# Up projection by channels with the norm root multiplied in the sums

## The reference

```python
h = rmsnorm(x, ffn_norm[l])                     # x: (1, 256, 2048)
u = causal_dwconv(jnp.einsum('bsd,df->bsf', h, w_up[l]), conv_w[l], conv_b[l])
gate, up = jnp.split(u, [D_FF], axis=-1)        # D_FF = 5632, w_up: (2048, 11264)
x = x + jnp.einsum('bsf,fd->bsd', jax.nn.silu(gate) * up, w_down[l])
```

## Time and profile before

| | us |
|---|---|
| median of 3 timed runs (2417.47 to 2429.39) | 2417.7 |
| profiled execution | 2424.76 |
| its span | 2423.0 |
| TensorE busy | 2336.9 |
| VectorE busy | 1652.8 |
| ScalarE busy | 1048.0 |
| one turn of the up loop, 569.3 to 665.8 | 96.5 |

### The profile page before, as it was taken

The page is one execution under the profiler, slowest core; times in us unless marked ns, Lnnn a source line. Parts: engine busy times, 40 slices in busy tenths (PEclk is TensorE's granted clock), DMA queues, the critical chain, the costliest instruction groups (busy, mean ns, idle before and its releaser), DMA issues.

```text
span 2423.0 us, 31984 instructions
## 1 busy us (share of the span) xinstructions
PE 2336.9 (96%) x11221; PEld 1935.5 (80%) x11221; DVE 1652.8 (68%) x2393; ACT 1048.0 (43%) x1506; POOL 75.1 (3%) x112
## 2 busy tenths in 40 slices
PE   8999999999999999999999999998999699899997
PEld 6778778878878788777888888887888699799976
DVE  5368866687787877777778585766758765466644
ACT  5576554555555555343452222223222625443433
POOL 1012110000000000000000000000000000000000
PEclk9999999999999999999999999999999899899999
DMA  7946544576766666777746464544646255312243
GB/s 242 196 149 197 178 133 154 175 233 200 234 210 216 223 219 207 237 246 239 250 157 208 140 197 142 183 155 157 224 159 219 79 180 172 113 61 74 69 145 133
DMA packets 225519, 430.39 MB, mean 178 GB/s; under 512 B 13799, under 2 KB 38623, under 8 KB 224128
## 3 DMA queue, kind: packets, MB, share of 16 engines
q1 hardware_dynamic: 222112, 418.96, 54.5%
q10 hardware_dynamic: 2720, 9.83, 1.2%
q0 software_dynamic: 576, 0.14, 0.0%
HBM read 426.16 MB, written 2.72 MB: 177 GB/s over the span
## 4 chain that ended last, share of the span: by engine, by line
PE 64%; issue 19%; DVE 7%; DMA 5%; ACT 4%; DVEq 0%; POOL 0%; SPq 0%; ACTq 0%; POOLq 0%
PE ps L600 38%; PE ps L634 11%; PE ps L611 9%; DMA raw<-in_w_down 3%; DVE lo L547 2%; ACT hi L543 2%; DVE ada_acc L576 2%; PE ps L650 1%; DVE ustage L1683 1%; DMA raw<-in_w_in 1%; PE ps L2295 1%; DMA xres<-in_x 1%; PE ps L2193 0%; PE ps L2045 0%; PE ps L2044 0%
## 5 line engine op out<-in xcount | busy, mean ns | idle before, releaser
L543 ACT ACTIVATE hi<-raw 128x1024 fp32r<-128x1024 f32 x604 | 635.6, 1059 | 1142.5 <-PE ps L600 540.6
L547 DVE TENSOR_TENSOR lo<-raw,hi 128x1024 fp32r<-128x1024 f32 x604 | 730.9, 1222 | 523.5 <-ACT hi L543 520.6
L576 DVE SCALAR_TENSOR_TENSOR ada_acc<-raw,csil,ada_acc 128x512 f32<-128x512 f32 x720 | 491.7, 746 | 2.4 <-DMA raw<-in_ada_w 2.4
L600 PE MATMUL ps<-hi,h_hi 128*128 128x512 f32 x960 | 383.0, 399 | 6.5 <-DVE lo L547 6.5
L600 PE MATMUL ps<-hi,h_lo 128*128 128x512 f32 x960 | 378.9, 395 | 0.0
L600 PE MATMUL ps<-lo,h_hi 128*128 128x512 f32 x960 | 378.8, 395 | 0.0
L600 PE MATMUL ps<-hi,g 128*128 128x512 f32 x704 | 227.8, 400 | 7.0 <-DVE lo L547 6.9
L600 PEld LDWEIGHTS ps<-hi,h_hi 128*128 128x128 f32 x960 | 180.8, 188 | 53.4 <-DVE lo L547 13.4
L600 PEld LDWEIGHTS ps<-hi,h_lo 128*128 128x128 f32 x960 | 180.8, 188 | 42.3
L600 PEld LDWEIGHTS ps<-lo,h_hi 128*128 128x128 f32 x960 | 181.0, 188 | 40.1
L600 PEld LDWEIGHTS ps<-hi,g 128*128 128x128 f32 x704 | 133.2, 189 | 43.0 <-DVE lo L547 12.0
(11 more groups left out here) (323 smaller groups left out, 3584.4 us busy)
## 6 DMA issues: line engine op xcount, KB each, us to landing
raw<-in_ada_w SPq DMA_DIRECT2D x192, 512.0 KB, 4.2
raw<-in_w_up SPq DMA_DIRECT2D x176, 512.0 KB, 4.5
raw<-in_w_down SPq DMA_DIRECT2D x88, 512.0 KB, 4.9
raw<-in_w_in SPq DMA_DIRECT2D x84, 512.0 KB, 4.4
raw<-in_pool_w_in SPq DMA_DIRECT2D x64, 512.0 KB, 4.1
raw<-in_mla_w_in SPq DMA_DIRECT2D x56, 448.0 KB, 3.9
raw<-in_w_out SPq DMA_DIRECT2D x32, 512.0 KB, 3.6
raw<-in_pool_w_out SPq DMA_DIRECT2D x32, 512.0 KB, 4.6
```

The lines of the kernel that those rows point to most:

```text
L543: act.activation(hi[:, slot, :, :], raw[:, slot, :, :], ACT.Copy).then_inc(hi_split, 1 + ada)
L547: dve.tensor_tensor(lo[:, slot, :, :], raw[:, slot, :, :], hi[:, slot, :, :].bitcast(F32), ALU.subtract).then_inc(lo_split, 1)
L576: ins = dve.scalar_tensor_tensor(acc, raw[:, slot, k, :], csil[:, v, kt:kt + 1], acc, ALU.mult, ALU.add)
L600: mm = pe.matmul(ps[:, bank, 0:n], a[:, kt0 + k, tok * P:(tok + 1) * P], w[:, slot, k, col0:col0 + n], start=first and k == 0 and s == 0, ...
```

## The change

The up projection keeps a 128x128 tile of the weights fixed and moves the 256 tokens of h: 24 matmuls of 256 columns a chunk. The result has channels on partitions, as the convolution needs it. Gate panels stay in banks 0 and 1 and up panels in 2 and 3 until their taps are done; a panel waits for the taps of the one before it in its banks. The staging and the transpositions are gone.

The norm root is needed as a row over tokens, the same on all partitions. VectorE makes two diagonal matrices from the root columns, TensorE multiplies them by a matrix of minus ones into bank 3 (before chunk 6 of gate panel 0), and VectorE copies that with the sign turned to `root_row`. Each finished panel is multiplied by it in place in PSUM (`scale_u`, one VectorE operation of 128x1024), and the taps read the scaled sums.

The down panels use banks 6, 0, 2, 0 (and the next), and the squares of the second norm of x go to a throw-away tile in SBUF.

```diff
+        root_diag = at(120)("root_diag", [P, TT, P])
+        root_row = at(128)("root_row", [P, SEQ])
+        x_junk = at(8)("x_junk", [P, W])
...
-        def turned_u(m):
-            return ps[:, 6 + m // 2, (m % 2) * SEQ:(m % 2 + 1) * SEQ]
+        def u_cols(which, m):
+            return ps[:, 2 * which + m // 2, (m % 2) * SEQ:(m % 2 + 1) * SEQ]
+        DOWN_BANKS = [6, 0, 2, 0]
...
+        def panel_by_channels(pe, first, i, order, j0, a_hi, a_lo, bank0, before=None):
+            for j in range(CH):
+                if before is not None:
+                    before(j0 + j)
+                at = first + place(order, j0 + j)
+                slot = at % RING
+                pe.wait_ge(lo_split, i * len(order) + at + RING + 1)
+                for k in range(CK_T):
+                    for n in range(W // P):
+                        for s, (w, a) in enumerate(((hi, a_hi), (hi, a_lo), (lo, a_hi))):
+                            mm = pe.matmul(ps[:, bank0 + n // 2, n % 2 * SEQ:(n % 2 + 1) * SEQ], w[:, slot, k, n * P:(n + 1) * P],
+                                           a[:, CK_T * j + k, :], start=j == 0 and k == 0 and s == 0 and n % 2 == 0,
+                                           stop=j == CH - 1 and k == CK_T - 1 and s == 2 and n % 2 == 1)
+                mm.then_inc(chunks_used, 1 + ada_behind(at))
...
-            def stage_u(n, which, used_chunks):
-                act.wait_ge(chunks_used, used_chunks)
-                act.wait_ge(g_lo_done, FREE + n) if which == 0 else act.wait_ge(gated, FREE + n)
-                for i in range(TT):
-                    ins = act.activation(ustage[:, which, i, :], ps[:, 2 * which + i, :], ACT.Identity, scale=x_stats(1)[2][:, i:i + 1])
-                ins.then_inc(u_staged[which], 1)
             def tap_two(i, which):
-                act.wait_ge(u_turned[which], i + 1)
+                act.wait_ge(u_scaled[which], i + 1)
+                act.wait_ge(g_lo_done, FREE + i) if which == 0 else act.wait_ge(gated, FREE + i)
...
-                stage_u(n, 1, done(CH))
...
-                    stage_u(n + 1, 0, done(2 * CH))
...
-                panel_squares(act, 2, i * 2, ps[:, 6, :])
+                panel_squares(act, 2, i * 2, x_junk[:, :])
...
+            def root_columns():
+                dve.wait_ge(x_root, 2)
+                for i in range(TT):
+                    dve.tensor_scalar(root_diag[:, i, :], ident, x_stats(1)[2][:, i:i + 1], None, ALU.mult).then_inc(root_diag_ready, 1)
+            def root_rows():
+                dve.wait_ge(root_spread, 1)
+                dve.tensor_scalar(root_row[:, :], ps[:, 3, 0:SEQ], -1.0, None, ALU.mult).then_inc(root_row_ready, 1)
+            def scale_u(which, used_chunks):
+                dve.wait_ge(chunks_used, used_chunks)
+                v = ps[:, 2 * which:2 * which + 2, :].rearrange("p a (b n) -> p (a b) n", n=SEQ)
+                dve.tensor_tensor(v, v, root_row[:, :].unsqueeze(1).to_broadcast([P, 4, SEQ]), ALU.mult).then_inc(u_scaled[which], 1)
...
                 older_taps(n, 0)
-                split(ahead(2), ahead(CH) if last else ahead(CH + 2))
+                split(ahead(2), ahead(CH))
+                scale_u(1, done(CH))
+                if not last:
+                    split(ahead(CH), ahead(CH + 2))
                 older_taps(n, 1)
...
                     split(ahead(CH + 4), ahead(2 * CH))
+                    scale_u(0, done(2 * CH))
...
-            los(dve, C_UP, 0, 0, 1 + RING, CH + RING)
+            los(dve, C_UP, 0, 0, 1 + RING, 4 + RING)
+            root_columns()
+            los(dve, C_UP, 0, 0, 4 + RING, CH + RING - 1)
+            root_rows()
+            los(dve, C_UP, 0, 0, CH + RING - 1, CH + RING)
+            dve.wait_ge(root_row_ready, 1)
+            scale_u(0, used(C_UP + CH))
...
             def gate_panel(n, first, i, order, j0, before=None):
-                pe.wait_ge(u_staged[0], FREE + n)
-                panel_by_tokens(pe, first, i, order, j0, h_hi, h_lo, pair(0), W, before=before)
+                pe.wait_ge(taps[0], FREE + n * 2)
+                panel_by_channels(pe, first, i, order, j0, h_hi, h_lo, 0, before)
...
+                if j == CH - 2:
+                    pe.wait_ge(root_diag_ready, TT)
+                    for i in range(TT):
+                        mm = pe.matmul(ps[:, 3, i * P:(i + 1) * P], negones, root_diag[:, i, :], start=True, stop=True)
+                    mm.then_inc(root_spread, 1)
...
+            pe.wait_ge(root_row_ready, 1)
...
-                        if j == j0 + CH + 2:
-                            turn_u(n, 1)
...
-            turn_u(N_UP - 1, 1)
...
+                    if i * 2 + half in (1, 2):
+                        pe.wait_ge(taps[2 - i * 2 - half], FREE + N_UP * 2)
+                    panel_by_tokens(pe, C_DOWN, i, DOWN_ORDER, half * n, g_hi, g_lo, [(tok, DOWN_BANKS[i * 2 + half] + tok) for tok in range(TT)],
+                                    W, FT, before=ada_before)
```

More of the change, by code:

```diff
@@ L518, in two_block_kernel @@
         attn_added, ffn_added = sem("attn_added"), sem("ffn_added")
-        u_staged = [sem("gate_staged"), sem("up_staged")]
-        u_turned = [sem("gate_turned"), sem("up_turned")]
+        u_scaled = [sem("gate_scaled"), sem("up_scaled")]
+        root_diag_ready, root_spread, root_row_ready = (sem(n) for n in ("root_diag_ready", "root_spread", "root_row_ready"))
         taps = [sem("gate_taps"), sem("up_taps")]
@@ L1152, in _ @@
             act.sem_inc(mla_taken, PAIR)
-            for s in (x_squared, u_staged[0], u_staged[1], g_hi_done):
+            for s in (x_squared, g_hi_done):
                 act.sem_inc(s, FREE)
@@ L1275, in _ @@
                     panel_squares(act, 1, n, x_squares[:, :])
-            def stage_u(n, which, used_chunks):
-                act.wait_ge(chunks_used, used_chunks)
-                act.wait_ge(g_lo_done, FREE + n) if which == 0 else act.wait_ge(gated, FREE + n)
-                for i in range(TT):
-                    ins = act.activation(ustage[:, which, i, :], ps[:, 2 * which + i, :], ACT.Identity, scale=x_stats(1)[2][:, i:i + 1])
-                ins.then_inc(u_staged[which], 1)
             def tap_two(i, which):
-                act.wait_ge(u_turned[which], i + 1)
+                act.wait_ge(u_scaled[which], i + 1)
+                act.wait_ge(g_lo_done, FREE + i) if which == 0 else act.wait_ge(gated, FREE + i)
                 for m in range(4):
                     ch = i * 4 + which * FT + m
-                    ins = act.activation(conv[which][:, m, :], turned_u(m), ACT.Identity,
+                    ins = act.activation(conv[which][:, m, :], u_cols(which, m), ACT.Identity,
                                          scale=cols[:, bass.ds(ch + V_CONV[2][0] * P + V_CONV[2][1], 1)],
@@ L1299, in up_and_gate @@
                 ahead = lambda j: place(order, j0 + j) + RING
-                done = lambda j: i * step + used(first + place(order, j0 + j))
                 his(act, first, i, step, ahead(0), ahead(2))
@@ L1320, in _ @@
             his(act, C_UP, 0, 0, 1 + RING, CH + RING)
-            act.wait_ge(x_root, 2)
-            stage_u(0, 0, used(C_UP + CH))
             with act.Fori(0, UP_TURNS) as i:
@@ L1350, in _ @@
                 act.wait_ge(ffn_added, i * 2 + 1 + PAIR + 1)
-                panel_squares(act, 2, i * 2 + 1, ps[:, 6, :])
+                panel_squares(act, 2, i * 2 + 1, x_junk[:, :])
                 if last:
@@ L1668, in _, with add_panel @@
                 los(dve, 0, 0, 0, first_at(c) + RING, first_at(c + 1) + RING)
-            def add_panel(done, c, half, col0):
+            def add_panel(done, c, n):
                 dve.wait_ge(chunks_used, c)
-                v = xres[:, :, bass.ds(col0, W)]
-                dve.tensor_tensor(v, ps[:, 2 - 2 * half:4 - 2 * half, :], v, ALU.add).then_inc(done, 1)
+                v = xres[:, :, n * W:(n + 1) * W]
+                dve.tensor_tensor(v, ps[:, DOWN_BANKS[n]:DOWN_BANKS[n] + TT, :], v, ALU.add).then_inc(done, 1)
+            def root_columns():
[9 more added lines that the diff above has]
+                dve.tensor_tensor(v, v, root_row[:, :].unsqueeze(1).to_broadcast([P, 4, SEQ]), ALU.mult).then_inc(u_scaled[which], 1)
             def older_taps(i, which):
@@ L1682, in older_taps @@
                         ch = i * 4 + which * FT + m
-                        ins = dve.scalar_tensor_tensor(conv[which][:, m, back:SEQ], turned_u(m)[:, 0:SEQ - back],
+                        ins = dve.scalar_tensor_tensor(conv[which][:, m, back:SEQ], u_cols(which, m)[:, 0:SEQ - back],
                                                        cols[:, bass.ds(ch + vec[0] * P + vec[1], 1)], conv[which][:, m, back:SEQ],
@@ L1690, in up_and_gate @@
                 ahead = lambda j: place(order, j0 + j) + RING
+                done = lambda j: i * len(order) + used(first + place(order, j0 + j))
                 split = lambda a, b: los(dve, first, i, len(order), a, b, ADA_UP, 1, 1)
@@ L1769, in _ @@
```

(18 more changed lines are left out.)

## The result

The changed kernel takes 2435.8 us (median of 8, 2434.6 to 2441.0), the kernel before 2418.7 (median of 8, 2417.0 to 2429.4): ratio 1.0068, 95% interval 1.0053 to 1.0082. It is 0.7% slower where no change was forecast. It still lies inside the stated range of 2405 to 2439, but only in the part that was left for the slower rivals; the forecast's own range ended at 2424. The profiled execution took 2441.0 us with a span of 2439.2, against a span of 2423.0 before.

The account below looks back on a forecast made before the run. TensorE, 96% busy, was taken as the bound, with VectorE setting two stretches a turn. Terms +0.6, +0.2 and 0 around the up loop and -1.3 at its end summed to -0.5 us: 2417 us, range 2405 to 2439.

Parts of the forecast that it names:

- the slower rivals: Up loop: code refetched at back edges (2434 us, chance 0.11), or 256-column pairs slower when held (2437 us, 0.12).
- the forecast's own range: Whole kernel, main forecast without rivals: 2411 to 2424 us, allowing a longer multiplication and a larger gain at the end.
- the second rival: Up loop's four back edges: TensorE waits for code to be fetched, +8 to +50 us, middle 2434 us; chance 0.11.
- seven blocks just fit: TensorE's instruction memory: the longer loop body, 6 or 7 blocks of 16 KB, fits within eight blocks.
- Matmuls 0.1185 us apart: Weight chunks: 24 matmuls of 256 columns take 2.84 us, 0.055 more each; +9.7 us where TensorE sets the pace.
- The third rival: Weight chunks: 256-column pairs slower in a held stream, at 0.125 us a pair; 2437 us, chance 0.12.
- Turns gone, gain swallowed by two stretches: Up loop: two of four removed transpositions gain nothing where VectorE sets the time; about +0.05 us a turn.
- The first rival: Up loop: TensorE alone sets the pace, so the two stretches shrink too; -13.8 us, 2404 us, chance 0.15.
- The multiplication 1.22 us, in a gap: VectorE, each of 22 panels: scaling by the root row takes 1.22 us, covered where VectorE now waits.
- The end of the stage, -1.3 us: After the last up panel: down panel starts at once, but the following DMA moves only from 988.4 by -1.3 us.
- the wait four chunks later: Early down stage: TensorE waits 2.5 us for a low half that stands behind VectorE's tap tail.
- Before the loop: Panel 0 and ten chunks +1.0, root matmuls +0.45, a transposition -0.87: +0.6 us before the first VectorE-set point.

Follow-up runs that it names:

- e5: Changed kernel with 102 already met waits added to TensorE's program far ahead of the up loop, moving its code 0.4 packet: 2418.8 us, ratio 1.0006.
- e1: Changed kernel with the up stage's loop written out on TensorE alone, other engines keeping theirs: 2419.3 us, ratio 0.9997.
- e7: Changed kernel, TensorE's loop written out, VectorE reordered: one low half between the two groups of older taps, product one low half later: 2402.1 us, ratio 0.9934.
- e10: Kernel before with only VectorE's order changed: a low half between the older tap groups, product one low half later: 2406.7 us, ratio 0.9949.
- e8: Changed kernel, TensorE's loop written out, multiplication by the root row cut to two elements: 2416.5 us, ratio 0.9997.
- e2: Kernel before with the up stage's loop written out on TensorE alone: 2418.0 us, ratio 0.9993.
- e3: Kernel before with one met-wait instruction added ahead of each weight-chunk matmul in TensorE's loop, body 1275 instructions: 2417.7 us, ratio 0.9987.
- e4: Kernel before with two met-wait instructions added ahead of each weight-chunk matmul in TensorE's loop, body 1660 instructions: 2426.8 us, ratio 1.0019.
- e6: Kernel before with TensorE's loop padded to 1660 instructions and moved 0.6 packet by 154 met waits ahead of it: 2445.8 us, ratio 1.0125.
- e9: Changed kernel with 256 met waits ahead of TensorE's up loop, moving its code one whole packet: 2434.1 us, ratio 1.0068.

## Why the prediction was wrong, point by point

**The step that failed** is the weighing of the second rival, *the loop no longer fits TensorE's instruction buffer*, by which the sum of the forecast has nothing for the four back edges. They cost 17.7 us: four turns of the changed kernel take 404.9 us, of e5 387.2, so 4.4 us an edge. The mechanism was written down with its place, its sign (idle at each turn's start, instruction packets in later turns) and nearly its price (+16 us in the middle, 4.0 an edge). The price is in part luck: the rival counted idle alone, which was 2.2 to 2.9 us ahead of the first pair. The rest of the 4.4 is a second idle of 0.4 to 0.7 us and, behind three of the four edges, the granted clock of 0.50, which it did not name; how the rest divides was not taken apart. The rival got a chance of 0.11. The grounds were that "seven blocks just fit" and that the body of before was kept. But the body's length was rounded to blocks, and whether it touches seven or eight depends on where it begins. With 6.2 blocks that is decided by the start, which nothing in the profile shows. The argument that was written there ("just fit") excluded nothing, and the rival should have weighed more.

**What each other step measured**, the fetch put aside (e5, e1):
- *Matmuls 0.1185 us apart.* Long runs give 216 in 25.76 us, 0.1193 (768 in 91.95, 0.1197, in e7): a chunk is 2.86 us, forecast 2.84. The third rival (0.125) is out.
- *Turns gone, gain swallowed by two stretches.* Right as an account: +0.05 us a turn forecast, +0.3 measured (96.80 against 96.54). There are 2.9 us of waits a turn, and TensorE restarts at 626.9, 650.4, 698.8 and 702.6 in e1's turn, behind the taps and the product. Right too in its ground: e7 moves only what stands in those stretches and the turn falls to 93.6. The first rival (*TensorE alone sets the pace*) is false for this order. In the order of e7 TensorE does set the pace, but there the kernel before gains too (e10), and the change is worth 5 us and not that rival's 14.
- *The multiplication 1.22 us, in a gap.* 1.224 by the page of after; e8 shows it hidden to within 0.4 us a turn (97.3 against 96.9).
- *The end of the stage, -1.3 us.* Mis-sized. From the end of the last up panel to the next modulation sums in the down stage:

```profile
969.31 25.76 PE ps L631 x216
...
1125.45 1.68 PE ps L671 x16
```

  that is 130.4 us; before it was 137.5 (973.42 to 1110.89), so -7.1 by these two traces. One trace each is too few: the six of the kernel before and its variants (e2, e3, e4, e6, e10) give 133.0 to 137.9, the seven of the changed kernel and its variants 129.3 to 134.2. The means are 4.0 us apart, which is the better figure for the term. The idle and the slow clock went as said, and the wait four chunks later came as said (2.7 us, forecast 2.5). What I had priced was the distance to one DMA; which of the loads behind it carry the rest I did not separate.
- *Before the loop.* From the start of gate panel 0 to the loop's first matmul the kernel before takes 23.2 us, e5 24.5 (442.77 to 467.28): +1.3, of which the sum had 0.9 (eight chunks at 0.055, the root matmuls 0.45). The other 0.4 is an idle at the loop's entry that the trace calls issue.

With the fetch put aside the forecast of 2417 against 2417.7 stands: e5 has ratio 1.0006, e1 0.9997. That it stands so closely is luck in part: four turns and the stretch before the loop cost some 1.3 us more than the sum has, and the end gives some 2.7 us more.

## What to carry to other kernels

When a change makes a loop's body on TensorE longer, count its instructions in blocks of 256 and look at every later turn for packets of code. With the bodies of 6.2 and 6.5 blocks here the start of the loop decided, so some hundred instructions of padding ahead of it, or writing the loop out, are worth trying before such a change is judged. And an engine that is 96% busy with a few listed waits can still be set by another's order of work: move long operations apart before removing work from the busy one.

## What the runs showed of the hardware

- The same body of about 1595 instructions is kept over a back edge or fetched again whole (8 or 9 packets of 16 KB a turn, 4.4 us of time) by its place in the code alone: moved by 102 instructions it was kept (e5), by 256 fetched again (e9).
- A gap of 2.2 us at the edge was followed by a granted clock of 0.50 for 3.2 us, beginning 1.6 us after work went on. At another edge of the same run 2.9 us of idle was followed by none of it (1.00 from 671.9 to 680).
- A wait that comes from code fetching can be listed as one for a low half that the next chunk does not need: two of four were.
- Met waits in the queue were free at one per matmul of 0.2325 us (e3) and came with a turn 1.4 us longer at two (e4).
